# Conditioned encoder layer: two of the six modulation rows before the attention and summed on VectorE, the others during the dilated steps; first norm turned four tiles to a bank

## What is computed

```python
cs  = silu(c)                                  # (1, 1024)
mod = cs @ w_ada + b_ada                       # (1, 6*1024): sh1, sc1, gt1, sh2, sc2, gt2
h   = rms_norm(x, g_mix) * (1 + sc1) + sh1
x   = x + gt1 * token_mixer(h, positions, w_in, sinks, w_branch_a, w_branch_b, w_out)
h   = rms_norm(x, g_ffn) * (1 + sc2) + sh2
x   = x + gt2 * hier_moe(h, w_group, b_group, w_route, b_route, w_gate, w_up, w_down)
out = rms_norm(x, g_final)
```

## Time and profile before

| | us |
|---|---|
| median of three runs (3032.02 to 3035.68) | 3035.41 |
| profiled execution | 3033.13 |
| its span | 3031.0 |
| PE busy | 2752.4 (91%) |
| DVE busy | 1731.7 (57%) |
| ACT busy | 1500.7 (50%) |
| POOL busy | 817.5 (27%) |

### The profile page before, as it was taken

One profiled execution on the slowest core, in us unless ns is written; L12 is line 12 of the kernel. 1 busy time (PEld: TensorE's weight loads), 2 busy tenths in 40 slices (PEclk: granted clock), 3 DMA queues, 4 the chain that ended last, 5 costly groups with the idle time before them and its releaser, 6 DMA issues.

```text
span 3031.0 us, 50427 instructions
## 1 busy us (share of the span) xinstructions
PE 2752.4 (91%) x14228; PEld 2316.2 (76%) x14229; DVE 1731.7 (57%) x3141; ACT 1500.7 (50%) x2615; POOL 817.5 (27%) x617
## 2 busy tenths in 40 slices
PE   8899999999999997899999799939999999999950
PEld 2399999999888786688888678727788888888840
DVE  3555655556677675645441143457866735365868
ACT  2455666766545444344432132216766634365854
POOL 1244444545422211334444211101211111111210
PEclk9999999999999998899999899959999999999985
DMA  7500000000000001334343343328987846476988
GB/s 269 201 24 25 25 24 24 25 25 25 21 19 17 11 10 59 124 127 139 131 131 113 125 171 143 138 111 308 378 311 271 318 165 228 145 280 255 390 318 328
DMA packets 195890, 451.20 MB, mean 149 GB/s; under 512 B 39958, under 2 KB 91158, under 8 KB 193772
## 3 DMA queue, kind: packets, MB, share of 16 engines
q1 hardware_dynamic: 176812, 389.46, 36.2%
q0 software_dynamic: 14400, 52.44, 4.7%
q10 hardware_dynamic: 4608, 8.39, 0.7%
HBM read 380.01 MB, written 70.21 MB: 149 GB/s over the span
## 4 chain that ended last, share of the span: by engine, by line
PE 73%; DVE 8%; issue 8%; DMA 6%; ACT 3%; POOL 1%; SPq 1%; DVEq 0%; ACTq 0%; POOLq 0%
PE bank L1691 14%; PE bank L1906 14%; PE bank L1790 5%; PE bank L1834 4%; PE S_ps L1917 3%; PE E_ps L1917 3%; PE O_ps L1756 3%; DMA sb_w_in<-in_w_gate_up 3%; PE S_ps L1790 3%; PE S_ps L1737 3%; PE E_ps L1790 3%; PE S_ps L1739 3%; PE bank L1657 2%; PE E_ps L1723 2%; PE S_ps L1834 1%
## 5 line engine op out<-in xcount | busy, mean ns | idle before, releaser
L1906 PE MATMUL bank<-sb_gu,sb_x_hiT 128*128 (+1 forms) x1568 | 493.4, 396 | 11.4 <-DVE sb_x_loT L1552 8.5
L726 POOL TENSOR_TENSOR sb_h_lo<-sb_hT,sb_h_hi 128x1024 fp32r<-128x1024 f32 x128 | 337.2, 2635 | 610.4 <-ACT sb_h_hi L841 610.4
L1691 PE MATMUL bank<-sb_w_hi,sb_h_hi 128*128 (+1 forms) x1024 | 401.8, 392 | 15.5 <-issue 9.1
L1906 PEld LDWEIGHTS bank<-sb_gu,sb_x_hiT 128*128 128x128 f32 x1568 | 293.4, 189 | 73.4 <-issue 11.0
L1691 PE MATMUL bank<-sb_w_hi,sb_h_lo 128*128 (+1 forms) x1024 | 344.5, 336 | 0.0
L1691 PE MATMUL bank<-sb_w_lo,sb_h_hi 128*128 (+1 forms) x1024 | 343.7, 336 | 0.0
L1538 DVE TENSOR_TENSOR sb_gu<-sb_w_in,sb_gu 128x1024 f32 (+1 forms) x256 | 301.1, 1220 | 64.2 <-ACT sb_gu L1071 62.4
L1071 ACT ACTIVATE sb_gu<-sb_w_in 128x1024 f32 (+1 forms) x256 | 257.1, 1059 | 104.8 <-DMA sb_w_in<-in_w_gate_up 80.5
L1906 PE MATMUL bank<-sb_gu,sb_x_loT 128*128 (+1 forms) x784 | 308.3, 393 | 0.0
L765 POOL TENSOR_TENSOR sb_g_lo<-sb_g_raw,sb_g_hi 128x1408 fp32r<-128x1408 f32 x64 | 212.5, 3342 | 341.3 <-ACT sb_g_hi L946 341.3
L1691 PEld LDWEIGHTS bank<-sb_w_hi,sb_h_hi 128*128 128x128 f32 x1024 | 193.7, 189 | 31.2 <-issue 19.1
(11 more groups left out here) (346 smaller groups left out, 6113.8 us busy)
## 6 DMA issues: line engine op xcount, KB each, us to landing
sb_w_in<-in_w_gate_up SPq DMA_DIRECT2D x256, 512.0 KB, 6.2
sb_w_in<-in_w_expert_down SPq DMA_DIRECT2D x128, 512.0 KB, 5.2
sb_g_raw<-in_w_gb SPq DMA_DIRECT2D x64, 704.0 KB, 4.1
sb_wada<-in_w_ada SPq DMA_DIRECT2D x24, 1024.0 KB, 8.0
sb_yp<-y_d SPq DMA_DIRECT2D x16, 1024.0 KB, 6.8
sb_w_raw<-in_w_qkv SPq DMA_DIRECT2D x128, 96.0 KB, 2.0
sb_x_round<-in_x SPq DMA_DIRECT2D x4, 2048.0 KB, 12.6
mT_d<-sb_mg ACTq DMA_DIRECT2D x32, 256.0 KB, 2.1
```

Of the source, the lines that this page charges most:

```text
L726: nc.gpsimd.tensor_tensor(h_lo[c][:], tile_src(g, T), h_hi[c][:].bitcast(F32), ALU.subtract).then_inc(sem("h_lo_ready"), 1)
L1691: last = nc.tensor.matmul(bank[c][:, 0:PASS_COLS].rearrange("p (a m) -> p a m", a=1), x[c][:, k, :], w[:, ds(row + k, 1), :], start=(k == ...
L1906: last = nc.tensor.matmul(PS[j][:].rearrange("p (a n) -> p a n", a=1), x[:, k, :], gu[:, ds(gu_row(e, part, k), 1), j * DE:(j + 1) * DE], ...
```

## The change

Two of the six rows (four chunks, `FIRST_MOD = 4`) are formed before the attention, and by another engine: DVE multiplies each 128x512 block of w_ada by its column of silu(c) and adds it to a sum (`add_chunk`), and PE adds the 128 partitions of that sum by four matmuls with a column of ones, which land as columns of the bank that A1 and B1 are read from (`mod_columns`). The bias and the norm's gain arrive as rows and are turned once by PE; so are the positions, which before came in by slow transfers of single elements.

The first norm is turned four tiles to a bank: for each of eight blocks PE turns the four tiles of a round into one 128x512 bank (seven banks in use), and DVE and ACT take the banks by turns (`take_blocks`). The rows of x are scaled in place by ACT (two rows of each of the rounds 0 to 2, three of round 3) and POOL (the others, `POOL_ROWS`). POOL also clamps the angles. The first pass's weights come in two transfers and are split in four pieces each by ACT and POOL (`raise_first`, `lower_first`), in place of sixteen.

The other eight chunks are formed during the 64 steps of dilated groups 0 and 1: SP loads one 128x512 block of w_ada a step, DVE adds it after the copies of the step (`late_add`), and after every eight steps PE adds the partitions by one matmul into bank 4 (which those steps leave free), DVE adds bias and gain (`late_take`), and SP stores the row. The steps of groups 0 and 1 are all written out, so that each can name its own block; groups 2 and 3 are looped as before.

```diff
 DVE, first stage
-        take_row(0)
-        dve.wait_ge(sem("pos_in"), 112)
+        dve.wait_ge(sem("pos_in"), 64)
+        nc.vector.tensor_copy(pos_rows[:], pos_rows_i[:]).then_inc(sem("pos_cast"), 1)
...
-        for j in range(NORM_FROM, MOD_CHUNKS):
-            take_row(j)
-            ch.join()
-            t = 2 * (j - NORM_FROM)
-            take_tile(t)
-            take_tile(t + 1)
-            if t % ROUND == 2 and t + 2 < TT:
-                row_stats(t // ROUND + 1)
+        row_stats(0)
+        dve.wait_ge(sem("c_silu"), 1)
+        add_chunk(0)
+        row_stats(1)
+        for j in range(1, FIRST_MOD):
+            add_chunk(j)
+        take_columns()
+        take_blocks(0)
+        take_blocks(1)
+        row_stats(2)
+        take_blocks(2)
+        row_stats(3)
+        take_blocks(3)
+        def add_chunk(j):
+            for k in range(KD):
...
+                acc, w, by = mod_sum[j % 2][:], wada[n % WADA][:, k % (KD // 2), :], c_sil[:, k:k + 1]
+                if k == 0:
+                    wait(dve, sem("mod_mm"), j - 1)
+                    ins = nc.vector.tensor_scalar(acc, w, by, None, ALU.mult)
+                else:
+                    ins = nc.vector.scalar_tensor_tensor(acc, w, by, acc, ALU.mult, ALU.add)
+        def take_blocks(q):
+            for k in range(0, KD, 2):
+                dve.wait_ge(sem("xT_done"), KD * q + k + 1)
+                nc.vector.tensor_scalar(hT[:, k, q * CHUNK:(q + 1) * CHUNK], turn_bank(KD * q + k), A1[:, k:k + 1], B1[:, k:k + 1], ALU.mult, ALU.add).then_inc(sem("h_all"), 1)
 PE, first stage
-        def mod_chunk(j):
-            wait(pe, sem("mod_row"), j - 1)
...
-                last = nc.tensor.matmul(out_row, c_sil[:, k:k + 1], wada[n % 4][:, k % (KD // 2), :], start=(k == 0), stop=False)
+        def mod_columns(j):
+            pe.wait_ge(sem("mod_added"), KD * (j + 1))
+            for c in range(CHUNK // P):
+                last = nc.tensor.matmul(bank[2][:, 4 * j + c:4 * j + c + 1], mod_sum[j % 2][:, c * P:(c + 1) * P], ones_col, start=True, stop=True)
+        mod_columns(0)
+        turn_blocks(0, range(TURN_BANKS))
+        for j in range(1, FIRST_MOD):
+            mod_columns(j)
+        turn_blocks(0, range(TURN_BANKS, KD))
+        for q in range(1, ROUNDS):
+            turn_blocks(q, range(KD))
 ACT, first stage
+        squares(0)
+        scale_rows(0)
+        squares(1)
+        scale_rows(1)
...
+        take_blocks(0)
+        squares(2)
+        scale_rows(2)
+        take_blocks(1)
+        squares(3)
+        scale_rows(3)
+        take_blocks(2)
+        for i in range(KD // 2):
+            raise_first(i)
+        take_blocks(3)
 POOL, first stage
+POOL_ROWS = ((1, 3), (1, 3), (1, 3), (3,))
+        scale_rows(0)
+        pool.wait_ge(sem("turned"), 1)
+        nc.gpsimd.tensor_scalar(ang[:], ang[:], lim, -lim, ALU.min, ALU.max).then_inc(sem("reduced"), 1)
+        for q in range(1, ROUNDS):
+            scale_rows(q)
...
+        for i in range(KD // 2):
+            lower_first(i)
 SP, first stage
+        x_in_round(0)
+        x_in_round(1)
+        for n in range(MOD_HALVES):
+            ada_half(n)
+        x_in_round(2)
+        x_in_round(3)
 steps of groups 0 and 1, all engines
-            for T in range(T0, T0 + 4):
+            end = T0 + TILES_PER_GROUP - 2
+            for T in range(T0, end if g < 2 else T0 + 4):
                 straight(T)
-            end = T0 + TILES_PER_GROUP - 2
-            if g < 3:
+            if g < 2:
+                pass
+            elif g < 3:
                 looped(g, T0 + 4, end, True)
 SP, step
+            if late_piece(T) is not None and T + 1 < LATE:
+                late_in(T + 1)
 DVE, step, between the copies (last.then_inc qk_ready) and the mask
+            if late_piece(T) is not None:
+                late_add(T)
+            if late_due(T, 3) is not None:
+                late_take(late_due(T, 3))
+        def late_add(m):
+            i, k = m // KD, m % KD
+            dve.wait_ge(sem(f"late_in{m % 2}"), 16 * (m // 2 + 1))
...
+            acc, w, by = late_sum[i % 2][:], late_w[m % 2][:], c_sil[:, k:k + 1]
+            if k == 0:
...
+                ins = nc.vector.tensor_scalar(acc, w, by, None, ALU.mult)
+            else:
+                ins = nc.vector.scalar_tensor_tensor(acc, w, by, acc, ALU.mult, ALU.add)
 PE, step, after the first four blocks of the projection
+            if late_due(T, 2) is not None:
+                i = late_due(T, 2)
+                pe.wait_ge(sem("late_added"), KD * (i + 1))
+                nc.tensor.matmul(PS[4][0:1, :], ones_col, late_sum[i % 2][:], start=True, stop=True).then_inc(sem("late_mm"), 1)
```

More of the change, by code:

```diff
@@ L48 @@
 assert PIECES == 2 * RING
-EARLY, LATE = range(KD // 2), range(KD // 2, KD)
+EARLY, LATER = range(KD // 2), range(KD // 2, KD)
 MOD_CHUNKS = N_MOD * D // CHUNK
-MOD_HALVES = 2 * MOD_CHUNKS
-MOD_LOADS = MOD_HALVES // 4
+MOD_HALVES = 2 * FIRST_MOD
+WADA = 3
+MOD_LOADS = (3, 3, 2, 0)
+XBUF = 3
+POOL_ROWS = ((1, 3), (1, 3), (1, 3), (3,))
+LATE_CHUNKS = MOD_CHUNKS - FIRST_MOD
+LATE = LATE_CHUNKS * KD
 OUT_LOADS = KD // 4
@@ L137, in body @@
     ident = keep("ident", [P, P])
-    ones_row = keep("ones_row", [1, 2])
+    columns = keep("columns", [P, 3])
+    ones_col, eps_col, half_pi = (columns[:, i:i + 1] for i in range(3))
+    c_sil = keep("c_sil", [P, KD])
     A1 = keep("A1", [P, KD])
@@ L391, in group_of, with turn_bank, late_piece, late_due @@
         return min(max(T, 0) // TILES_PER_GROUP, 3)
+    TURN_BANKS = 7
+    def turn_bank(n):
+        return PS[(0, 1, 3, 4, 5, 6, 7)[n % TURN_BANKS]][:]
+    def late_piece(T):
+        return T if isinstance(T, int) and 0 <= T < LATE else None
+    def late_due(T, after):
+        if isinstance(T, int) and T - after >= KD - 1 and (T - after) % KD == KD - 1 and (T - after) // KD < LATE_CHUNKS:
+            return (T - after) // KD
+        return None
     def schedule(eng, step):
@@ L864, in _, with scale_rows @@
-        squares(0)
+                t = ROUND * q + r
+                wait(act, sem("sumsq"), t)
+                nc.scalar.activation(sq1[:], x_round[q % XBUF][:, r, :], ACT.Square, accum_out=ssq1[:, t:t + 1]).then_inc(sem("sumsq"), 1)
+            act.wait_ge(sem("sumsq"), ROUND * (q + 1))
+            at = slice(ROUND * q, ROUND * (q + 1))
+            nc.scalar.activation(rms1[:, at], ssq1[:, at], ACT.Sqrt, bias=eps_col, scale=1.0 / D).then_inc(sem("rms"), 1)
+        def scale_rows(q):
+            act.wait_ge(sem("rstd"), q + 1)
+            for r in range(ROUND):
+                if r not in POOL_ROWS[q]:
+                    row = x_round[q % XBUF][:, r, :]
+                    nc.scalar.activation(row, row, ACT.Copy, scale=rstd1[:, ROUND * q + r:ROUND * q + r + 1]).then_inc(sem("xn_act"), 1)
@@ new lines, in take_blocks, with raise_first @@
+        def take_blocks(q):
+            act.wait_ge(sem("columns"), 1)
+            for k in range(1, KD, 2):
+                act.wait_ge(sem("xT_done"), KD * q + k + 1)
+                nc.scalar.activation(hT[:, k, q * CHUNK:(q + 1) * CHUNK], turn_bank(KD * q + k), ACT.Identity, bias=B1[:, k:k + 1], scale=A1[:, k:k + 1]).then_inc(sem("h_all_act"), 1)
+        def raise_first(i):
+            act.wait_ge(sem(f"w_in{i // 2}"), 16)
+            rows = slice(2 * i, 2 * i + 2)
+            nc.scalar.activation(w_hi[:, rows, :], w_first[:, rows, :], ACT.Copy).then_inc(sem("w_hi_ready"), 4)
@@ new lines, in turn_blocks @@
+        def turn_blocks(q, ks):
+            pe.wait_ge(sem("xn_pool"), sum(len(rows) for rows in POOL_ROWS[:q + 1]))
+            pe.wait_ge(sem("xn_act"), sum(ROUND - len(rows) for rows in POOL_ROWS[:q + 1]))
+            for k in ks:
+                n = KD * q + k
+                if n >= TURN_BANKS:
+                    pe.wait_ge(sem("h_all_act" if (n - TURN_BANKS) % 2 else "h_all"), (n - TURN_BANKS) // 2 + 1)
+                for r in range(ROUND):
+                    last = nc.tensor.transpose(turn_bank(n)[:, r * P:(r + 1) * P], x_round[q % XBUF][:, r, k * P:(k + 1) * P], ident[:])
+                last.then_inc(sem("xT_done"), 1)
@@ new lines, in _ @@
+        pe.wait_ge(sem("g_in"), 32)
+        nc.tensor.transpose(bank[2][:, 2 * TT:2 * TT + 3 * KD], vec_rows[:], ident[0:3 * KD, 0:3 * KD])
+        pe.wait_ge(sem("pos_cast"), 2)
+        nc.tensor.transpose(bank[2][:, 0:TT], pos_rows[:], ident[0:TT, 0:TT])
+        by_r = pos_4[:].rearrange("b (i r) -> b r i", r=4)
+        for r in range(4):
+            last = nc.tensor.transpose(bank[2][:, TT + 4 * r:TT + 4 * r + 4], by_r[:, r, :], ident[0:4, 0:4])
+        last.then_inc(sem("vectors_turned"), 1)
```

276 lines of the change are left out of this document (137 added, 139 removed).

## The result

| us | before | changed |
|---|---|---|
| median, 4 runs each | 3035.55 (3032.02 to 3038.29) | 3005.14 (3004.46 to 3006.95) |
| ratio, 95% interval | | 0.9901 [0.9884, 0.9919] |
| span of the profiled execution | 3031.0 | 3002.7 |
| first projection on PE | 140.68 | 89.70 |
| groups 0 and 1, 64 steps | 430.5 | 446.9 |

An eviction is ScalarE's first copy of a tile's projection out of PSUM, one in each of the 128 steps; steps are counted from the start of one to the start of the next.

A forecast was written before the change was run, and what follows sets the result against it. A loading stage bound by TensorE's modulation chunks, not bytes, then dilated steps with TensorE full. 3033.1 - 57.2 (first stage) - 10.9 (straight steps) + 7.0 (row sums) + 28 (adds against GpSimd) = 3000 us; range 2964 to 3026.

The forecast's parts named there:

- the rivals: Four alternatives: port free (2972, chance 0.17), first stage poor (3019, 0.08), ring every step (3036, 0.08), slower (3072, 0.05).
- part 1: First stage, up to the first projection: it starts at 83.5 us instead of 140.68, -57.2 us.
- part 2: Dilated groups 0 and 1: written-out steps take 6.59 us each, 419.6 us instead of 430.5, -10.9 us.
- part 3: Dilated groups 0 and 1: one TensorE row sum per eight steps, 0.87 us each, +7.0 us.
- part 4: Dilated groups 0 and 1: VectorE's late adds wait behind GpSimd's subtraction at the shared SBUF port, +28 us.
- the sum: All terms together, 3000 us; within part 1, ScalarE's listed work after t0, 35 us, plus 2 for TensorE's turns.
- the poor first stage: Rival, chance 0.08: first stage gives less, VectorE's adds and GpSimd not overlapping, TensorE turning at half clock; 3019 us.
- t0: First stage: the moment the columns A1 and B1 exist, forecast at 41 to 51 us, taken as 46.5.
- the second rival: First stage gives less: adds and GpSimd don't overlap, 128 blocks turned at half clock (+14), t0 51; 3019 us, chance 0.08.
- The ring: Dilated steps: late add, mask to exponentials, ScalarE's h_hi and GpSimd's h_lo wait in a circle, 6.9 or 8.3 us.
- the gap: VectorE's 1.45 us idle time before the mask in a dilated step, said to absorb late_take (0.69, twice 1.4 us).

The follow-up runs named there:

- experiment 1: Kernel before, with only the steps of dilated groups 0 and 1 written out straight instead of looped: 3024.17 us, ratio 0.9967.
- experiment 2: Changed kernel with the late sum kept in a PSUM bank, in SBUF only after the eighth block: 2983.13 us, ratio 0.9834.
- experiment 8: Changed kernel with the late sum in PSUM and each of the eight late row sums done twice: 2993.23 us, one run.
- experiment 12: Kernel before, unchanged, profiled a second time: one run of 3039.47 us, with 1875.5 us behind the 128th eviction against 1868.6 in its first profile.
- Experiment 5: Changed kernel with GpSimd scaling two rows of x instead of seven, ScalarE the others: 2998.29 us, ratio 0.9888.
- experiment 3: Changed kernel with the late add moved ahead of the copies, behind the rotary multiplies, sum still in SBUF: 2987.27 us, ratio 0.9843.
- experiment 4: Changed kernel with seven of eight late adds cut to one column, most later modulation rows left out: 2970.03 us, ratio 0.9787, steps 438.5 us.

## Why the prediction was right, and where its sizes were off

The range (2964 to 3026) holds 3005.1, the mechanism is the one forecast, and none of the rivals came true as told. Its terms, from the two profiles:

| term | forecast | measured | from |
|---|---|---|---|
| part 1, to the first projection | -57.2 | -51.0 | 89.70 against 140.68 |
| part 2, straight steps | -10.9 | -10.6 | experiment 1 |
| part 3, eight row sums | +7.0 | +9.0 | 8 x 1.13, experiments 2 and 8 |
| part 4, adds against GpSimd | +28 | +19 | 446.9 - 419.9 - 7 x 1.13 |
| the rest | 0 | +5 | +5.9 behind the 128th eviction, not shown to be the change's (experiment 12) |

That the sum came within 5 us of the result is luck in part: part 4 was 9 us too dear, and parts 1 and 3 and the rest came out 6, 2 and 5 us worse than forecast. The range's top isn't worked out either: the poor first stage that it is said to take in gives 3019.

**Part 1** was too good by 6 us, nearly all in t0: the columns were ready at 51.8, outside the 41 to 51 that I gave. I started VectorE's sum at 8 us and summed its work alone. By that the adds begin at 17; the first started at 20.34, and before it stand 1.22 us of waiting for the root of round 0 and 1.0 for w_ada's first half, since the order puts the reciprocal first and x ahead of w_ada. An add takes 0.76 and comes every 0.79 us, not 0.69. And seven of those from 20.86 to 35 ran 0.88 to 1.84 us beside masks, scaled rows and the clamp, 4.3 us in all; the 7.5 us that I had taken for GpSimd were more than that and hid part of the rest. From the last add to A1 and B1 pass another 2.5 us (eight PE instructions of 1.88 at 49.30, then three small ones of VectorE), which I counted nowhere.

From t0 on it took 37.9 against 37. ScalarE's order needed 34.0 us from its first take to the end of h_hi (51.86 to 85.88), where the sum has 34.4. GpSimd scales a row in 2.84 us (61.28, two rows in 5.67), a price that I had nowhere; on ScalarE's path it shows only as the waits for rstd (0.24 and 2.25 us, 2 in the sum). Its four w_lo pieces (7.1 us) push h_lo back by 1.2, counted nowhere either. Experiment 5 takes five of the seven rows from GpSimd and gets 3.1 us, 2.2 before t0 and 0.9 behind.

Part of the second rival came true with it: t0 passed its 51 (though adds and GpSimd did overlap, at a loss of 4.3 us), and TensorE turned some blocks at its lower clock. After 7.76 us without work, eight turns took 1.97 us at 67.00 with a granted clock of 0.50 (66 to 71 us), against 1.03. But the rival's +14 priced all 128 blocks as if each were on the path; the two slow groups of eight that the chain shows there (1.97 at 67.00, 1.71 at 68.97) cost 1.6 us by my estimate.

**Part 3.** 0.87 came from matmuls in a row; the marginal cost is 0.83, but one that stands alone costs 1.13.

**Part 4** is the port, as forecast: experiments 2, 3 and 4 change the operand, the place and the size, and only the size leaves the wait. The Trainium skill, "SBUF — State Buffer", section "Who interferes with whom", says that VectorE with at most one SBUF input, outside its two-port modes, does not contend with GpSimd; by it the adds of experiment 2 had to run at their own 0.74, and they do (0.746). The size of the ring was overstated. Group 0 pays 1.3 us (213.2, less experiment 1's 208.5 and three row sums), not 6; group 1 pays 18 (233.7, less 211.3 and four row sums), not 22. In group 0 most adds are held as well (1.8 to 2.4 us each), but there the steps have room for it. The steps of group 1 take turns, but 6.97 and 7.38, a mean of 7.18 instead of 7.3; 6.6 and 8 did not alternate. I had let one long step clear the way for a whole free one; in fact POOL's start slides by a part. That each pair takes 14.35 us I can measure but not derive. The two gain rows (L1401, 2.66 us in the mean, both inputs in SBUF) are some 2.5 of the 19; I had put them in the gap at nothing. Experiment 2 leaves them, and its 430.5 less 419.9 is 7.9 of row sums and 2.5 of these (steps of 7.63 and 7.65 us, and 6.78 and 6.81 behind them).

What would have shown it wrong did not come: no step above 7.6 in the mean, no projection after 95. What I gave for a right one held in kind but not in three sizes: first projection 79 to 89 (89.70), steps of 6.6 and 8 by turns (6.97 and 7.38), and at most 7.5 for a step, with a row sum (7.72 for most of these, and 8.26 and 8.29 for the two steps with a gain row).

## What to carry to other kernels

A reduction moved to VectorE beside a busy GpSimd can be held for as long as GpSimd's instruction lasts, whatever the add itself lasts: cutting the add to one column saved only 8 of 19 us, while an idle PSUM bank as accumulator saved 16. When the bound on an engine is summed, its first wait belongs in the sum: an in-order engine that first serves someone else's input starts when that arrives. And before a load is moved forward, look at who reads the load that it passes.

## What the runs showed of the hardware

- A 128x1 instruction of VectorE with two SBUF inputs is held for a whole 128x1024 subtraction of GpSimd (2.25 us against 0.21 free; mean of 56: 1.31 us). The 128x512 `tensor_scalar` from SBUF to SBUF is held too (1.78 us in the mean of 8), but into PSUM it isn't (0.75). A `scalar_tensor_tensor` with one input in SBUF and one in PSUM isn't held, whether it writes to PSUM (746 ns) or to SBUF (737 ns).
- GpSimd takes 2.84 us to scale 128x1024 fp32 by a column, and 2.34 us to subtract two arrays of that size: the operation with fewer inputs is the slower. ScalarE scales it in 1.14.
- The mask instructions of GpSimd (bf16, 128x256) took 400 ns each before and 719 ns in the changed kernel, where VectorE's angles run beside them; VectorE's 128x1536 instruction went from 1.76 to 1.87 us.
